# Sparse attention's start: bias table in two head groups, the first scores ahead of the compression, the root ahead of gelu, biases one head ahead

## The chip, the cores and the metric

One core of a Trainium2 chip runs the whole program. The metric is device time in microseconds (us) of one execution; three executions of the kernel before gave 3542.86, 3545.63 and 3548.09, median 3545.63.

## What is computed

Three layers of a decoder, all in fp32: a first block with a recurrent branch and sparse attention beside each other, then two blocks more. The change lies in the sparse attention of the first block alone (256 tokens, 16 heads of 64 in four key groups):

```python
kc = compress(k_c, pe_k, w1_k, w2_k)      # gelu(windows of 32 tokens @ w1) @ w2, 15 windows
vc = compress(v_c, pe_v, w1_v, w2_v)
s_c = einsum('bsgrd,bngd->bgrsn', q, kc) * scale + bias_c    # compressed scores
p_c = softmax(where(valid_c, s_c, NEG_INF)) * any_c
o_c = einsum('bgrsn,bngd->bsgrd', p_c, vc)
s = einsum('bgrqk', qc, ks) * scale + bias[rel_bucket(dist)] # selected blocks: all four of them here
o_s = softmax(where(dist >= 0, s, NEG_INF)) @ vs
o_w = ...                                                     # window attention, the same form
o = gate0 * o_c + gate1 * o_s + gate2 * o_w
```

With 256 tokens every block is selected and the window covers all, so a head has two score tables of 256 by 256 (causal: 128 + 256 columns for two blocks of queries), and one compressed table of 256 by 15. The recurrent branch ends in an RMS norm (a sum of squares over eight tiles, a root, a reciprocal, a scaling), and both branches go into the product with w_out.

## The kernel before, in words

The program is one list of instructions for each engine, tied by semaphores. The large products take their weights in quarters of 128x1024: SyncE loads a quarter (`w_raw`), ScalarE rounds it (`w_hi`, function `hi`), VectorE subtracts (`w_lo`, function `lo`), TensorE uses both; each step waits for the step ahead and for its buffer (four quarters deep). The pair of weight tiles `in1` makes the projections; the two pairs of `cmp` (c0 and c0 + 1) hold the first weights of the key and the value compression; `out1` is the product behind attention.

Between `in1` and `out1` the order is written by hand:

- SyncE loads the bias table `bias` (128 x 16 heads x 384, 3 MB from a Toeplitz copy in HBM, eight DMAs) behind all eight quarters of `cmp`. Its place was the input of `in1`, so it waits until that is used up.
- TensorE turns the values to tokens, multiplies 96 small products of the compression (m0, m1), turns the gelu results (`turn_hidden`), sums the squares of the recurrent branch (`lru_sum`), makes the scores of head pair 0 (`pair_scores`), the second compression product, and the compressed scores of all heads. `keep_busy` is a row of products whose result nobody reads.
- ScalarE rounds the quarters, squares the recurrent tiles, then gelu (`hidden`), the copies of it, the root of the norm, and a table of exp. Each change of function family loads a table.
- VectorE adds biases to the scores of a head (two instructions of 128x384), takes maxima (two), and negates them; ScalarE takes exp of the head (four instructions with sums); VectorE then makes the reciprocal and the factor and scales the head in place; TensorE transposes it; ScalarE copies it (`pt_att`); after each pair TensorE multiplies with the values (`pair_results`). This is a loop over `it`, written out on all three engines: in step `it` VectorE scores head `it` and scales head `it` - 1. In step 0 VectorE also does the whole softmax of the compressed scores (`compressed`).

`lru_n` and `z` are tiles of the recurrent branch, `s_first` and `s_more` the scores of even and odd pairs, `p_cmp` the compressed scores, `stat` small statistics. Score banks hold one pair: m0 and m1, and bank0 and bank1.

## Time and profile before

| | us |
|---|---|
| median of three executions | 3545.63 |
| lowest, highest | 3542.86, 3548.09 |
| the profiled execution's own time | 3545.68 |
| its span | 3543.9 |
| from the start of the compression products to the first product of `out1` | 249.99 to 342.31 |

The stage that the change touches is less than 100 us of the span. Elsewhere TensorE's large products set the time; here the engines hand small work to each other, so it must be read from the order of time, the waits and the chain. `SPq` is SyncE's queue. `x4` at the end of a row is the number of instructions in it, and what stands in brackets is the idle time before and what ended it. An fp32 product appears as two instructions, and four exps of a head as eight (each with a read of its sum).

### The profile page before, as it was taken

To read this page: it belongs to the slowest core of one execution; us is meant where nothing else is said; L and a number is where in the kernel's file an instruction comes from. 1 tells how busy PE (TensorE), PEld (TensorE's weight loads), DVE (VectorE), ACT (ScalarE), POOL (GpSimd) and SP (SyncE) were. 2 spreads that over 40 slices of the span, in tenths; PEclk is the share of its full clock that TensorE was granted. 3 is DMA by queue.
4 is the path that set the end of the run, shared out by engine and by line. 5 is a ranking of instruction groups with operands and counts; after the bars stand their busy time and mean duration, and the time that the engine had idled before them with its cause. 6 is when DMAs were issued, how large, how long until landed. Compare 5 with 4: busy or idle time off the path is not lost.

```text
span 3543.9 us, 62898 instructions
## 1 busy us (share of the span) xinstructions
PE 3438.5 (97%) x21968; PEld 2998.0 (85%) x21968; DVE 2297.3 (65%) x3449; ACT 1788.3 (50%) x2742; POOL 489.5 (14%) x538
## 2 busy tenths in 40 slices
PE   9998999999999999999999999999489999999999
PEld 7886888888888888887888888888378888888888
DVE  5788565555555766775666677778855765565565
ACT  4477464545454554553555444444444554444454
POOL 0001410111114100123100001105012000001105
PEclk9999999999999999999999999999899999999999
DMA  6562545565556555553456556667235455555555
GB/s 212 172 184 61 190 151 192 186 191 185 190 183 194 170 188 170 162 168 119 145 193 197 187 189 196 202 222 246 59 125 186 147 190 191 185 187 193 181 187 195
DMA packets 190644, 626.52 MB, mean 177 GB/s; under 512 B 26822, under 2 KB 40328, under 8 KB 190360
## 3 DMA queue, kind: packets, MB, share of 16 engines
q1 hardware_dynamic: 179948, 612.29, 53.9%
q10 hardware_dynamic: 10572, 12.56, 1.2%
q8 instruction: 80, 1.31, 0.2%
q14 instruction: 44, 0.36, 0.0%
HBM read 620.32 MB, written 3.15 MB: 176 GB/s over the span
## 4 chain that ended last, share of the span: by engine, by line
PE 88%; DVE 7%; ACT 2%; DMA 1%; issue 1%; POOL 0%; SPq 0%; ACTq 0%; DVEq 0%; POOLq 0%
PE bank L1943 54%; PE bank L1946 28%; PE m L1966 1%; DVE w_lo L1073 1%; DMA w_raw<-stream 1%; PE m L1956 1%; PE m L1968 1%; DVE prod L1749 1%; ACT w_hi L481 0%; DVE st L1752 0%; DVE st L1754 0%; DVE y L1100 0%; DVE w_lo L1077 0%; ACT s_first L666 0%; ACT u_own L972 0%
## 5 line engine op out<-in xcount | busy, mean ns | idle before, releaser
L1073 DVE TENSOR_TENSOR w_lo<-w_raw,w_hi 128x1024 fp32r<-128x1024 f32 x1086 | 1336.4, 1253 | 776.5 <-ACT w_hi L481 770.2
L1943 PE MATMUL bank<-act,w_hi 128*128 128x512 f32 x6016 | 1512.8, 393 | 3.6 <-DVE w_lo L1073 1.6
L481 ACT ACTIVATE w_hi<-w_raw 128x1024 fp32r<-128x1024 f32 x1090 | 1129.5, 1054 | 409.8 <-PE bank L1946 362.6
L1943 PEld LDWEIGHTS bank<-act,w_hi 128*128 128x128 f32 x6016 | 1082.7, 189 | 204.6 <-DVE w_lo L1073 4.3
L1946 PEld LDWEIGHTS bank<-act,w_lo 128*128 128x128 f32 x6016 | 820.8, 190 | 58.9
L1946 PE MATMUL bank<-act,w_lo 128*128 128x256 f32 x6016 | 838.7, 282 | 0.0
L1943 PE MATMUL bank<-ffn,w_hi 128*128 128x512 f32 x2432 | 613.5, 393 | 4.0 <-DVE w_lo L1077 2.7
L490 ACT ACTIVATE low<-bank 128x256 f32<-128x256 f32 x542 | 207.5, 383 | 745.0 <-PE bank L1946 744.1
L1943 PEld LDWEIGHTS bank<-ffn,w_hi 128*128 128x128 f32 x2432 | 436.2, 189 | 83.2 <-DVE w_lo L1077 5.0
L1946 PEld LDWEIGHTS bank<-ffn,w_lo 128*128 128x128 f32 x2432 | 333.9, 190 | 25.1
L1081 DVE TENSOR_TENSOR ev<-bank,low 128x256 f32<-128x256 f32 x468 | 198.2, 423 | 236.7 <-ACT low L490 233.3
L1946 PE MATMUL bank<-ffn,w_lo 128*128 128x256 f32 x2432 | 341.5, 282 | 0.0
L1852 POOL TENSOR_TENSOR ffn<-fv,ffn 128x256 f32 x152 | 113.4, 746 | 1547.8 <-ACT ffn L738 1123.0
L1867 POOL TENSOR_TENSOR y<-y,ev 128x256 f32 (+1 forms) x109 | 92.3, 847 | 369.9 <-DVE ev L1081 369.9
L1835 POOL TENSOR_TENSOR sq<-y 128x256 f32<-128x256 f32 x90 | 95.2, 1058 | 315.9 <-DVE y L1786 226.6
L738 ACT ACTIVATE ffn<-fv 128x256 f32 (+1 forms) x88 | 36.8, 418 | 148.4 <-DVE fv L1389 148.4
L1837 POOL TENSOR_TENSOR ssum<-ssum,sq 128x256 f32<-128x256 f32 x90 | 105.9, 1177 | 7.1
L1966 PE MATMUL m<-act,w_hi 128*128 128x512 f32 x224 | 84.3, 458 | 4.0 <-DVE act L1197 2.5
L735 ACT ACTIVATE sg<-ev 128x256 f32<-128x256 f32 x88 | 36.9, 419 | 96.3 <-DVE ev L1384 96.3
L1077 DVE TENSOR_TENSOR w_lo<-w_raw,w_hi 128x768 fp32r<-128x768 f32 x58 | 67.9, 1187 | 21.5 <-ACT w_hi L486 21.2
L1384 DVE TENSOR_TENSOR ev<-ev,rms 128x256 f32<-128x256 f32 x176 | 74.8, 425 | 6.0
L1081 DVE TENSOR_TENSOR y<-bank,low 128x256 f32 (+1 forms) x74 | 31.4, 424 | 64.6 <-ACT low L490 64.6
(425 smaller groups left out, 2236.8 us busy)
## 6 DMA issues: line engine op xcount, KB each, us to landing
w_raw<-stream SPq DMA_DIRECT2D x1148, 512.0 KB, 3.5
b_part<-s_bt ACTq DMA_DIRECT2D x16, 256.0 KB
bias<-toeplitz SPq DMA_DIRECT2D x4, 512.0 KB, 9.1
pow_b<-powers ACTq DMA_DIRECT2D x8, 256.0 KB
pow_b<-powers ACTq DMA_DIRECT2D x16, 128.0 KB
res<-x_t SPq DMA_DIRECT2D x2, 512.0 KB, 9.0
res<-x_t ACTq DMA_DIRECT2D x2, 512.0 KB, 11.0
bias<-toeplitz SPq DMA_DIRECT2D x4, 256.0 KB, 11.7
```

Of the source, the lines that this page charges most:

```text
L481: a(w_hi[:, q, :], w_raw[:, q, :], ACT.Copy).then_inc(hi_ready, 1)
L490: a(low[:, w, 0:n], src[w][:, n:2 * n], ACT.Copy).then_inc(low_copied, 1)
L1073: e.tensor_tensor(w_lo[:, q, :], w_raw[:, q, :], w_hi[:, q, :].bitcast(F32), ALU.subtract).then_inc(lo_ready, 1)
L1081: e.tensor_tensor(dst, src[w][:, 0:n], low[:, w, 0:n], ALU.add).then_inc(drained, 1)
L1384: e.tensor_tensor(ev[:, w, :], ev[:, w, :], rms[:, :], ALU.mult).then_inc(sem(("gate_scaled", "up_scaled")[w]), 1)
L1835: e.tensor_tensor(sq[:, k % 2, :], y[:, k, :], y[:, k, :], ALU.mult).then_inc(y_squares, 1)
L1837: e.tensor_tensor(ssum[:, :], ssum[:, :], sq[:, k % 2, :], ALU.add).then_inc(y_squares, 1)
L1852: e.tensor_tensor(ffn[:, tile, T:2 * T], fv[:, w, :], ffn[:, tile, 0:T].bitcast(F32), ALU.subtract).then_inc(f_ready, 1)
L1867: e.tensor_tensor(y[:, 2 * i + w, :], y[:, 2 * i + w, :], ev[:, w, :], ALU.add).then_inc(y_acc, 1)
L1943: mm(bank[w][:, 0:2 * n], w_hi[:, q, wt], x(h * hk + k, 0, 2 * n), start=(h == 0 and k == 0), stop=False)
L1946: last = mm(bank[w][:, n:2 * n], w_lo[:, q, wt], x(h * hk + k, 0, n), start=False, stop=(h == 1 and k == hk - 1))
L1966: mm(m[w][:, :], w_hi[:, 2 * w + h, wt], act[:, k, :], start=(k == 0), stop=False)
```

## The change

- `bias` is loaded in two groups of heads: heads 0 to 3 directly behind the first quarter of the second `cmp` pair, heads 4 to 15 behind its fourth. The first group counts on the semaphore `bias_steps`, which the load of `rev_hot` now uses too.
- TensorE makes the scores of pair 0 ahead of the compression products, those of pair 1 behind the sums; the compression writes to one bank (m4), the gate transposes to m5. Three of the eight squares are summed ahead of the last quarter, five behind it. The compressed scores are made in two halves, around the transposes of head 0. `keep_busy(22)` and `keep_busy(10)` are gone.
- ScalarE takes the root of the recurrent norm ahead of gelu, and loads the table of exp ahead of the copies of gelu's results. The copies of the compressed keys and values come behind exp of head 0, exp of the compressed scores behind exp of head 3.
- VectorE scores head 0 ahead of the loop and head `it` + 1 in step `it`. The softmax of the compressed scores is cut in two, in steps 2 and 3. `lo(c0, 3)` and `lo(c0 + 1, 0)` move ahead of one other instruction each.
- The transposes of the compressed weights (`cmp_weights`) come behind heads 2, 3, 5, 7, ... 15 instead of 0, 2, 4, ... 14.

```diff
+    FIRST_HEADS = 4
+    TURN_AFTER = (2,) + tuple(range(3, NH, 2))
...
-            with sp_eng.Fori(2, after_in1) as i:
+            with sp_eng.Fori(2, after_in1 - 1) as i:
                 for q in range(4):
                     sp_eng.wait_ge(lo_ready, 4 * i + (q - 3))
                     load(i, q)
-            sp_eng.wait_ge(halves_used, 4 * PH["in1"][1])
-            sp_eng.wait_ge(sem("toep_out"), 16)
-            for lo_c, hi_c, off in ((128, 384, 127), (0, 128, 255)):
-                for p0 in range(0, P, ROWS):
-                    src = bass.AP(toeplitz.tensor, off - p0, [[383, ROWS], [384 * ROWS, NH], [1, hi_c - lo_c]])
-                    sp_eng.dma_start(bias[p0:p0 + ROWS, :, lo_c:hi_c], src).then_inc(sem("bias_loaded"), 16)
+
+            def load_bias(h0, h1, into):
+                for lo_c, hi_c, off in ((128, 384, 127), (0, 128, 255)):
+                    for p0 in range(0, P, ROWS):
+                        src = bass.AP(toeplitz.tensor, off - p0 + 384 * ROWS * h0,
+                                      [[383, ROWS], [384 * ROWS, h1 - h0], [1, hi_c - lo_c]])
+                        sp_eng.dma_start(bias[p0:p0 + ROWS, h0:h1, lo_c:hi_c], src).then_inc(into, 16)
+
+            for q in range(4):
+                sp_eng.wait_ge(lo_ready, 4 * (after_in1 - 1) + (q - 3))
+                load(after_in1 - 1, q)
+                if q == 0:
+                    sp_eng.wait_ge(halves_used, 4 * PH["in1"][1])
+                    sp_eng.wait_ge(sem("toep_out"), 16)
+                    load_bias(0, FIRST_HEADS, sem("bias_steps"))
+            load_bias(FIRST_HEADS, NH, sem("bias_loaded"))
...
+            hi(c0 + 1, 0)
             block_high(1)
...
-                a(hid_t[:, kv, :], m[kv][0:NG * NCMP, 0:T], ACT.Gelu_apprx_tanh).then_inc(sem("hid_ready"), 1)
+                a(hid_t[:, kv, :], m[4][0:NG * NCMP, T * kv:T * kv + T], ACT.Gelu_apprx_tanh).then_inc(sem("hid_ready"), 1)
...
-            hi(c0 + 1, 0)
+            hi(c0 + 1, 1)
+            hi(c0 + 1, 2)
             lru_square(0, 3)
-            hi(c0 + 1, 1)
-            lru_square(3, 6)
-            hi(c0 + 1, 2)
-            lru_square(6, 8)
             hi(c0 + 1, 3)
+            lru_square(3, 8)
+            root_table()
+            norm("lru", z, 8, lru_n, LT * P, None)
             hidden(0)
             hidden(1)
             a(counted[:, 0:1], eps_col[:, :], ACT.Copy).then_inc(low_copied, 4)
+            a(exp_use[:, :], eps_col[:, :], ACT.Exp)
             for kv in range(2):
                 s.wait_ge(sem("cmp_mm"), kv + 1)
                 a(hid[:, kv, :, :], m[2 + kv][:, 0:2 * NG * NCMP].rearrange("p (f n) -> p f n", f=2), ACT.Copy).then_inc(sem("cmp_cp"), 1)
-            root_table()
-            s.wait_ge(sem("blk_ready"), 1)
-            s.wait_ge(sem("cmp_mm"), 3)
-            for h in range(2):
-                pr = slice(64 * h, 64 * h + 64)
-                a(k_cmp[pr, :, h, :], m[4][pr, 0:60].rearrange("p (a h n) -> p a h n", a=2, h=2)[:, :, h, :],
-                  ACT.Copy).then_inc(sem("cmp_cp"), 1)
-            a(v_cmp[:, :], m[4][0:NCMP, 64:320], ACT.Copy).then_inc(sem("cmp_cp"), 1)
-            norm("lru", z, 8, lru_n, LT * P, None)
-            a(exp_use[:, :], eps_col[:, :], ACT.Exp)
+
+            def compressed_copies():
+                s.wait_ge(sem("blk_ready"), 1)
+                s.wait_ge(sem("cmp_mm"), 3)
+                for h in range(2):
+                    pr = slice(64 * h, 64 * h + 64)
+                    a(k_cmp[pr, :, h, :], m[4][pr, 0:60].rearrange("p (a h n) -> p a h n", a=2, h=2)[:, :, h, :],
+                      ACT.Copy).then_inc(sem("cmp_cp"), 1)
+                a(v_cmp[:, :], m[4][0:NCMP, 64:320], ACT.Copy).then_inc(sem("cmp_cp"), 1)
 
...
-                if hh % 2 == 0:
-                    s.wait_ge(sem("pct_mm"), hh // 2 + 1)
-                    a(pt_cmp[:, (hh // 2) % 2, :, :], m[5][0:NCMP, :].rearrange("n (h t) -> n h t", h=2),
+                if hh in TURN_AFTER:
...
                 if it == 0:
+                    compressed_copies()
+                if it == 3:
                     s.wait_ge(sem("cmp_vec"), 3)
...
             block_low(0)
+            c0 = PH["cmp"][0]
+            lo(c0, 3)
             v.wait_ge(sem("lru_act"), 4)
             v.wait_ge(sem("lru_vec"), 12)
             e.tensor_tensor(z[:, 0:LT, :], lru_i[:, :, :], z[:, LT:2 * LT, :], ALU.mult).then_inc(sem("lru_vec"), 1)
-            c0 = PH["cmp"][0]
-            lo(c0, 3)
+            lo(c0 + 1, 0)
             block_low(1)
-            lo(c0 + 1, 0)
             for q in range(1, 4):
...
             e.memset(counted[:, 1:2], 0.0).then_inc(drained, 4)
 
...
                 e.tensor_tensor(pc, pc, stat[:, 0:32].unsqueeze(2).to_broadcast([P, 32, NCMP]), ALU.subtract).then_inc(sem("cmp_vec"), 2)
+
+            def compressed_weights():
+                pc = p_cmp[:, :, :]
                 v.wait_ge(sem("cmp_exp"), 1)
...
-                v.wait_ge(sem("tok_cp"), 3)
...
+            def score(hh):
+                if hh == 0:
+                    v.wait_ge(sem("bias_steps"), 16 + 32 * P // ROWS)
+                if hh == FIRST_HEADS:
+                    v.wait_ge(sem("bias_loaded"), 32 * P // ROWS)
+                if hh >= 4:
+                    v.wait_ge(sem("pt_mm"), 2 * hh - 6)
+                for at_ in range(2):
+                    v.wait_ge(sem("s_mm"), 4 * (hh // 2) + 2 * at_ + hh % 2 + 1)
+                    e.scalar_tensor_tensor(s_att(hh)[:, at_, :], score_bank[hh % 2][at_][:, 0:384], HD ** -0.5, bias[:, hh, :],
...
+            v.wait_ge(sem("tok_cp"), 3)
+            score(0)
+            top(0)
+            top_negated(0)
             for it in range(NH + 1):
...
+                o = (it + 1) % 2
+                if it + 1 < NH:
+                    score(it + 1)
                 if it:
                     v.wait_ge(sem("att_exp"), it)
                     e.reciprocal(stat[:, 112 + 8 * o:116 + 8 * o], stat[:, 96 + 8 * o:100 + 8 * o]).then_inc(sem("att_inv"), 1)
-                if it < NH:
-                    v.wait_ge(sem("s_bias"), 2 * it + 2)
-                    e.tensor_reduce(stat[:, 80 + 8 * b:82 + 8 * b], s_att(it)[:, :, 0:128], AX.X, ALU.max).then_inc(sem("att_top"), 1)
-                    e.tensor_reduce(stat[:, 82 + 8 * b:84 + 8 * b], s_att(it)[:, :, 128:384], AX.X, ALU.max).then_inc(sem("att_top"), 1)
+                if it + 1 < NH:
+                    top(it + 1)
                 if it:
                     v.wait_ge(sem("att_inv"), it)
...
-                if it == 0:
-                    compressed()
+                if it + 1 < NH:
+                    top_negated(it + 1)
+                if it == 3:
+                    compressed_weights()
                 if it == 3:
                     lo(c0 + 2, 0)
...
+                if it == 2:
+                    compressed_scores()
                 if it == 3:
...
+            pe.wait_ge(sem("lru_sig"), 2 * LT)
+            pair_scores(0)
...
+                into = m[4][0:60, T * kv:T * kv + T]
+                for q in range(4):
+                    if kv and q == 3:
+                        pe.wait_ge(sem("tok_cp"), 3)
+                        lru_sum(0, 3)
+                    pe.wait_ge(lo_ready, 4 * i + q + 1)
...
+            lru_sum(3, 8)
+            pair_scores(1)
...
             turn_hidden(0)
-            lru_sum(0, 2)
             turn_hidden(1)
-            pair_scores(0)
             pe.wait_ge(sem("cmp_cp"), 2)
-            pe.wait_ge(sem("tok_cp"), 3)
...
                               cols[:, w2v + 64 * f:w2v + 64 * f + 64], start=(f == 0), stop=(f == 1))
             last.then_inc(sem("cmp_mm"), 1)
-            lru_sum(2, 8)
-            pe.wait_ge(sem("cmp_cp"), 5)
...
                 for j in range(NH // 2):
                     last = mm(m[4][:, 30 * (8 * b + j):30 * (8 * b + j + 1)], z[:, 16 + j, 128 * b:128 * b + 128],
                               k_cmp[:, j // 4, :, :].rearrange("p h n -> p (h n)"), start=True, stop=True)
-            last.then_inc(sem("cmp_scores"), 1)
-            keep_busy(22)
+                if b:
+                    last.then_inc(sem("cmp_scores"), 1)
 
...
             def transposes(hh):
-                if hh == 1:
-                    keep_busy(10, m[4])
...
             for it in range(NH + 2):
+                if it == 1:
+                    compressed_scores(0)
+                if it and it % 2 == 0 and it + 2 < NH:
+                    pair_scores(it // 2 + 1)
                 if 1 <= it <= NH:
-                    if it % 2:
-                        cmp_weights(it // 2)
+                    if it - 1 in TURN_AFTER:
+                        cmp_weights(TURN_AFTER.index(it - 1))
                     transposes(it - 1)
-                if it % 2 == 0 and it + 2 < NH:
-                    pair_scores(it // 2 + 1)
+                if it == 1:
+                    compressed_scores(1)
                 if it == NH:
```

On **SyncE**, between the last quarters of `cmp` and those of `out1`. Before:

```order
L405 DMA w_raw<-stream 128x1024
L422 REGISTER_ALU
L422 COMPARE_AND_BRANCH
L431 DMA bias<-toeplitz 32x16x256 x4
L431 DMA bias<-toeplitz 32x16x128 x4
L432 UNCONDITIONAL_BRANCH
L432 ISA
L405 ISA
L405 DMA w_raw<-stream 128x1024
```

And in the change:

```order
L407 DMA w_raw<-stream 128x1024
L424 REGISTER_ALU
L424 COMPARE_AND_BRANCH
L407 DMA w_raw<-stream 128x1024
L434 DMA bias<-toeplitz 32x4x256 x4
L434 DMA bias<-toeplitz 32x4x128 x4
L407 DMA w_raw<-stream 128x1024 x3
L434 DMA bias<-toeplitz 32x12x256 x4
L434 DMA bias<-toeplitz 32x12x128 x4
```

A quarter of 0.5 MB, then eight DMAs of four heads (0.75 MB), the three other quarters, then eight of twelve heads (2.25 MB).

On **ScalarE**, from gelu of the compression (`hid_t`) to the first exp. Before:

```order
L631 ACT_TABLE_LOAD
L631 ACTIVATE hid_t<-m 60x256 x2
L645 ACTIVATE counted<-eps_col 128x1
L648 ACTIVATE hid<-m 128x120 x2
L525 ACT_TABLE_LOAD
L525 ACTIVATE no_use<-eps_col 128x1
L654 ACTIVATE k_cmp<-m 64x2x15 x2
L656 ACTIVATE v_cmp<-m 15x256
L514 ACTIVATE rms<-m,eps_col 128x256
L658 ACT_TABLE_LOAD
L658 ACTIVATE exp_use<-eps_col 128x1
L666 ACTIVATE s_first,stat<-s_first,stat 128x128
```

And in the change, from behind the last square:

```order
L537 ACT_TABLE_LOAD
L537 ACTIVATE no_use<-eps_col 128x1
L526 ACTIVATE rms<-m,eps_col 128x256
L644 ACT_TABLE_LOAD
L644 ACTIVATE hid_t<-m 60x256 x2
L658 ACTIVATE counted<-eps_col 128x1
L659 ACT_TABLE_LOAD
L659 ACTIVATE exp_use<-eps_col 128x1
L662 ACTIVATE hid<-m 128x120 x2
L679 ACTIVATE s_first,stat<-s_first,stat 128x128
```

The root (`rms`) stood behind everything of the compression and now stands ahead of gelu; the tables come in the order root, gelu, exp instead of gelu, root, exp. The copies of `k_cmp` and `v_cmp` have gone behind exp of head 0.

On **TensorE**, behind the compression products. `hid_t` is turned, `hid` and `cols` are the second product, `k_cmp` makes the compressed scores, L2027 is `keep_busy`. Before:

```order
L2151 MATMUL m<-hid,cols 128x60 x2
L2154 MATMUL m<-cols,hid 15x64 x8
L2121 MATMUL m<-lru_n,ones 128x256 x6
L2161 MATMUL m<-k_cmp,z 128x30 x16
L2027 MATMUL m<-ident,ones 128x128 x22
L2132 MATMUL m<-z 128x256
L2132 MATMUL bank<-z 128x256
```

And in the change:

```order
L2187 MATMUL m<-ident,hid_t 128x60 x4
L2194 MATMUL m<-hid,cols 128x60 x2
L2197 MATMUL m<-cols,hid 15x64 x8
L2204 MATMUL m<-k_cmp,z 128x30 x8
L2229 MATMUL m<-ident,s_first 128x128 x6
L2204 MATMUL m<-k_cmp,z 128x30 x8
L2142 MATMUL m<-z 128x256
L2142 MATMUL bank<-z 128x256
```

The sums (L2121 before) have gone ahead of these rows, the compressed scores come in two halves with head 0's transposes between them, and nothing keeps the array busy.

On **VectorE**, around the second half of the compressed softmax. Before (in step 0):

```order
L1350 TENSOR_SCALAR stat<-stat 128x4
L1310 SCALAR_TENSOR_TENSOR p_cmp<-m,bias_cmp 128x480
L1312 TENSOR_REDUCE stat<-p_cmp 128x32
L1314 TENSOR_TENSOR p_cmp<-p_cmp,stat 128x480
L1316 TENSOR_REDUCE stat<-p_cmp 128x32
L1317 RECIPROCAL stat<-stat 128x32
L1320 TENSOR_SCALAR g_tok<-g_tok,cols 128x16
L1321 TENSOR_TENSOR stat<-stat,g_tok 128x32
L1323 TENSOR_TENSOR p_cmp<-p_cmp,stat 128x480
L1335 SCALAR_TENSOR_TENSOR s_first<-bank,bias 128x384 x2
L1338 RECIPROCAL stat<-stat 128x4
```

And in the change (in step 3):

```order
L1381 TENSOR_TENSOR stat<-stat,g_tok 128x4
L1362 TENSOR_SCALAR stat<-stat 128x4
L1335 TENSOR_REDUCE stat<-p_cmp 128x32
L1336 RECIPROCAL stat<-stat 128x32
L1337 TENSOR_SCALAR g_tok<-g_tok,cols 128x16
L1338 TENSOR_TENSOR stat<-stat,g_tok 128x32
L1340 TENSOR_TENSOR p_cmp<-p_cmp,stat 128x480
L1089 TENSOR_TENSOR w_lo<-w_raw,w_hi 128x1024
L1394 TENSOR_TENSOR s_more<-s_more,stat 128x2x128
L1394 TENSOR_TENSOR s_more<-s_more,stat 128x2x256
```

The five instructions that end with the write of `p_cmp` now stand behind the bias and the maxima of head 4, ahead of the scaling of head 2 (`s_more`).

## Rows read from the trace of the kernel before

**Rows 1.** The page of the kernel before: its head and the shares of the chain.

```profile
span 3543.9 us, 62898 instructions
...
PE 88%; DVE 7%; ACT 2%; DMA 1%; issue 1%; POOL 0%; SPq 0%; ACTq 0%; DVEq 0%; POOLq 0%
```

**Rows 2.** The chain that ended last, 236 to 345 us: start, length, what.

```profile
249.93 2.20 DVE z L1298
...
254.03 0.35 SPq L431
...
262.51 10.29 DMA bias<-toeplitz
...
282.23 1.87 ACT s_first L666 x8
```

**Rows 3.** Waits, 236 to 345 us: in total, times, longest.

```profile
DVE s_first L1335 <- DMA bias<-toeplitz: 11.5, 1, 11.5
...
ACT s_first L666 <- DVE stat L1350: 9.2, 4, 4.5
```

**Rows 4.** Order of time on TensorE: start, length, operation, idle before.

```profile
246.63 1.09 PE L2095 MATMUL m<-ident,z 128*128 128x128 f32 x8 [1.88 <-DVE z L1213]
...
249.99 0.47 PE L2112 MATMUL m<-w_hi,blk_s 128*60 128x256 f32 x1 [2.26 <-DVE blk_s L1293]
...
263.61 0.28 PE L2114 MATMUL m<-w_hi,blk_s 128*60 128x256 f32 x1
...
268.35 2.86 PE L2121 MATMUL m<-lru_n,ones 128*128 128x256 f32 x12
...
271.04 3.65 PE L2161 MATMUL m<-k_cmp,z 128*128 128x30 f32 x32
```

**Rows 5.** Order of time on ScalarE, the same columns.

```profile
261.38 0.38 ACT L631 ACTIVATE hid_t<-m 60x256 f32<-60x256 f32 x1
...
271.25 0.47 ACT L514 ACTIVATE rms<-m,eps_col 128x256 f32<-128x256 f32 x1 [1.92 <-PE m L2121]
...
271.74 1.28 ACT L658 ACT_TABLE_LOAD   x1
...
273.03 0.20 ACT L658 ACTIVATE exp_use<-eps_col 128x1 f32<-128x1 f32 x1
...
275.20 0.40 ACT L666 ACTIVATE s_first<-s_first,stat 128x128 f32<-128x128 f32 x1 [1.97 <-DVE stat L1350]
```

**Rows 6.** Order of time on VectorE, the same columns.

```profile
272.83 1.02 DVE L1335 SCALAR_TENSOR_TENSOR s_first<-m,bias 128x384 f32<-128x384 f32 x2 [11.50 <-DMA bias<-toeplitz]
...
273.89 0.42 DVE L1341 TENSOR_REDUCE stat<-s_first 128x2 f32<-128x256 f32 x1
...
274.23 0.68 DVE L1342 TENSOR_REDUCE stat<-s_first 128x2 f32<-128x512 f32 x1
...
277.79 0.65 DVE L1316 TENSOR_REDUCE stat<-p_cmp 128x32 f32<-128x480 f32 x1 [0.67 <-ACT p_cmp L698]
...
335.27 0.18 DVE L1338 RECIPROCAL stat<-stat 128x4 f32<-128x4 f32 x1 [1.00 <-ACT s_more L666]
...
335.69 1.03 DVE L1359 TENSOR_TENSOR s_more<-s_more,stat 128x256 f32<-128x256 f32 x2
```

**Rows 7.** Stretches: length, then PE, PEld, DVE, ACT, POOL busy, granted clock, DMA, GB/s.

```profile
251.00:252.00 1.00, 1.00 (x7) 1.00 (x6) 1.00 (x1) 0.66 (x2) 0.00 (x0) 0.50 0.87 336
...
254.00:255.00 1.00, 1.00 (x7) 1.00 (x7) 0.92 (x2) 1.00 (x3) 0.00 (x0) 0.60 0.60 66
...
277.00:278.00 1.00, 1.00 (x6) 1.00 (x6) 0.33 (x2) 0.67 (x2) 0.00 (x0) 0.50 0.00 0
...
290.00:291.00 1.00, 0.00 (x0) 0.00 (x0) 1.00 (x3) 1.00 (x5) 0.00 (x0) 1.00 0.00 0
...
293.00:294.00 1.00, 1.00 (x8) 0.62 (x10) 1.00 (x4) 0.00 (x0) 0.00 (x0) 0.50 0.16 45
...
295.02:302.25 7.23, 6.42 (x58) 4.29 (x54) 7.05 (x21) 7.09 (x24) 0.00 (x0) 0.95 0.00 1
```

83 lines of the change are left out of this document (42 added, 41 removed).

## The prediction

> **What bounds the kernel now.** I read the page's chain first: 88% of it is TensorE [rows 1], so over the span only TensorE's rate and its waits count. The change lies in less than 100 us between two large products, so I then read the chain inside that stage [rows 2], the waits [rows 3] and the order of time on three engines [rows 4 to 6]. One wait stands out: VectorE stands 11.5 us in front of the first biased score, until the bias table is there at 272.83 [rows 3, 6]. The chain goes back from it over the transfer (10.29 us behind the last of eight issues) to SyncE's first bias issue at 254.03 [rows 2]. That issue stands behind the last quarter of `cmp`, which waits for the low part of c0's last quarter, and this is behind the 2.20 us product on `z` [rows 2].
>
> Is the wait worth 11.5 us? Only if everything else that head 0 needs is there sooner. ScalarE takes the root at 271.25 and loads the table of exp until 273.02 [rows 5]. So with the table in place at once, exp of head 0 (275.20 before) could start at 273.2 at best: 2.0 us, and the rest of the 11.5 us is cover for ScalarE's and TensorE's chain. More can come only from edits that shorten that chain.
>
> Behind the start, the loop over heads fills two engines: in 7.23 us (two heads) VectorE is busy 7.05 and ScalarE 7.09 [rows 7]. Nothing of it can be gained by order, only its beginning and its end. ScalarE's waits for VectorE (9.2 us in four waits) [rows 3] lie at the beginning, and cost something only where VectorE itself isn't full.
>
> **Term A, the start of exp of head 0.** The compression products start when the first low part of `blk_s` is there; nothing ahead of that moves, so they start near 250 again [rows 4]. The scores of pair 0 now stand in the 2.26 us in which TensorE waits there [rows 4]: free. The products end at 263.9 [rows 4]. Eight sums are to be made before the root, six of which take 2.69 us (268.35 to 271.04) [rows 4], so 0.45 each and 3.6 for all: three ahead of the last quarter, five behind it, all on TensorE's path. End: 267.5. Then ScalarE: root 0.47, table of gelu 1.28, two gelus of 0.38, a small copy and the table of exp with its first use, 1.48, two copies of about 0.2 (all but the last in [rows 5]): 4.3 us, so 271.8. Against 275.20 that is 3.4 us earlier. A further gain is possible: the first products run at the lower level of the clock (granted 0.50 at 251, which is 1.2 GHz, and rising within the microsecond at 254) [rows 7], after 1.88 and 2.26 us of idle [rows 4]. With pair 0's scores in one of these gaps the clock may rise as early as 251, over 3 us sooner, which gives back half of that, 1.7 us (an estimate from these two rows). Bounds of A: 3.4 to 5.1 us; I take 4.3, the middle, since no row shows this stretch filled.
>
> The root's move puts two table loads into the open between the root and the first exp, where one stood before; that is in the sum. ScalarE's row shows 1.28 us for a load, and the next instruction starts 0.01 us behind it [rows 5]. The Trainium skill ("ScalarE: Activation LUTs", What ACT_TABLE_LOAD costs) puts a switch at about 2.66 us, since a drain of 1.38 comes on top. This speaks against the change: by it A would be smaller by 2.8 us; the trace shows no such drain, and the sum goes by the row.
>
> **Term B, from exp of head 0 to the end of the last scaling.** Before: 275.20 to 336.72, 61.5 us [rows 5, 6]. VectorE works through almost all of it: from 272.83 to 336.72, 63.9 us, of which it idles 0.67 for exp of the compressed scores, 1.00 for the last head [rows 6] and 0.18 in each pair of heads [rows 7], with smaller pieces about 3.1. So it has 60.8 us of work. Ahead of the end of exp of head 0 it can now do three heads' biases (1.06 each) and two heads' maxima (1.10) [rows 6]: 5.4. With exp itself (1.87) [rows 2] the stretch is 1.9 + 55.4 = 57.3 at the least, 4.2 less than before, if VectorE never waits again.
>
> It will wait, at three places. In step 3 exp of the compressed scores now stands behind exp of head 3 on ScalarE, and VectorE asks for it right behind the maxima of head 4; queued behind that wait are the low part for `out1`, the scaling of head 2 and so head 2's transposes: about 1.5 us (it was 0.67 behind head 0) [rows 6]. In steps 15 and 16 VectorE has no head left to score, and two scalings come faster than ScalarE can deliver two exps with their copies; I take 2.5 us for 1.00 before [rows 6]. In the steps with a high part on ScalarE the transposes now stand behind the next pair's scores, which delays copies and the next exp: some 1.6 us over four pairs. Sum 5.6, and B is 57.3 + 5.6 = 62.9: a loss of 1.4. Bounds: gain 4.2, loss 3.
>
> **Term C, the clock of TensorE.** The change takes 32 filler products out. Before, after the compressed scores (30 columns a product, 3.65 us) [rows 4] the clock fell: 0.50 granted at 277, although TensorE was busy throughout [rows 7]. It fell again to 0.50 at 293, behind an idle stretch at 290 [rows 7]. In the change TensorE meets: a wait for two gelus behind the root, one for the copies, one for the copies of the keys (behind exp of head 0), the same products of 30 columns in two halves, then a wait of some 6 us from head 1's transposes to the compressed weights. I expect a low clock from about 272 on. On the path of heads 0 and 1 TensorE has the second product, the compressed scores and two heads' transposes, some 6.5 us; if half is caught, it grows by 3.2, of which VectorE has about 0.8 to spare: a loss of 2.4. Bounds: 0 and 4.2 (all caught, some saved elsewhere). Before, the drop at 277 lay on fillers alone and cost nothing.
>
> The Trainium skill ("TensorE: Matmul & The Clock Gate", Part 1) says that "the default state is throttled, and activity releases the throttle"; by it C would be at its upper bound, since the activity here is thin. The row at 277, a fall in the middle of filler after thin products, agrees.
>
> **The transfers.** Bias group one (0.75 MB) starts some 8 us sooner than 254.03, right behind one quarter, and is there long before 261. Three quarters now stand behind its eight issues on SyncE; the first issues took 0.35 us [rows 2], so they come 3 to 4 us later. ScalarE wants them from 255.4 on: tight, but covered, as TensorE is the one that ends last there. Group two is issued from about 252.5, 1.5 us before the whole table was before, with a quarter less in it; head 4 asks for it at about 280. No cost.
>
> **Sum.** -4.3 + 1.4 + 2.4 = -0.5 us. On the profiled execution's 3545.68 (span 3543.9 [rows 1] and what lies around it), which lies at the median of 3545.63, this gives **3545.2 us**.
>
> **The rivals.**
> - *The clock holds* (C = 0, A = 5.1): -5.1 + 1.4 = -3.7, 3542.0. For it: the products at 271 to 274.5 ran at full clock while it lasted [rows 4]. Against it: the new waits. 0.22.
> - *VectorE never waits* (A = 5.1, B = -4.2): -9.3, 3536.4; with half of the three waits -6.5, 3539.2. For it: VectorE is the fuller engine before. Against it: ScalarE is as full [rows 7]. 0.12, of which 0.08 is below 3538.5.
> - *A low clock in the loop*, slower than before. TensorE is busy 6.42 of 7.23 us in a pair of heads [rows 7]; its work now comes in one piece, transposes, results and next scores, with one idle piece of 2 to 3 us instead of several short ones, as long as those behind which the clock fell [rows 4, 7]. A low stretch like that from 251 to 254 costs half its length, 1.7 us, since the next scores then come late for VectorE. It decides from the second such stretch on: two give -0.5 + 3.4, 3548.6; four 3552. 0.18, of which 0.05 is above 3552.7.
> - *The quarters come late* behind the eight issues, by up to 3 us, on TensorE's path: 3548.2. 0.04.
> - The forecast has what is left, 0.44, with 3543 to 3547.5 as its own range.
>
> **The range.** From half of "never waits" to three low stretches: 3538.5 to 3550.5; the three executions themselves lie 5.2 us apart. About 0.2% (7.1 us) is what a measurement of this kernel can tell from no change. Faster by more than that (under 3538.5): 0.08. Slower (over 3552.7): 0.06. Within: 0.86.
>
> **What would show it.** Right if in the profile after: the 11.5 us wait for the table is gone and VectorE's longest wait in the stage is for exp of head 0, 4 us or more; that exp starts between 270 and 272; VectorE waits 1 to 2 us for exp of the compressed scores and 2 to 3 for the last head; the granted clock is 0.50 somewhere between 272 and 290; the first product of `out1` starts within 2 us of 342.3. Wrong if ScalarE waits over 1 us for a quarter near 256 (transfers), if the loop has several microseconds at 0.50 (third rival), or if it ends before 338 (second rival).

## The result: 8 us slower

Median time after: 3553.28 us (13 runs, 3549.2 to 3557.56), before in the same comparison: 3545.07 us (13 runs). Ratio 1.0023, 95% interval 1.0015 to 1.0030: slower by 8.2 us (5.3 to 10.6). Forecast were 3545.2 us and a range of 3538.5 to 3550.5, so the time lies outside it. In the comparison of the last four runs below, one execution of the kernel before took 4245.9 us at a mean granted clock of 0.749 (0.988 to 0.993 in the others), and it is left out of every difference. Page of the profile of the kernel after, head and shares of the chain [rows 1]:

```profile
span 3551.3 us, 62764 instructions
...
PE 89%; DVE 6%; ACT 2%; DMA 2%; issue 1%; POOL 0%; ACTq 0%; SPq 0%; DVEq 0%; POOLq 0%
```

Waits of the kernel after, 244 to 356 us: in total, times, longest [rows 3].

```profile
ACT pt_cmp L687 <- PE m L2217: 10.0, 4, 3.5
ACT pt_att L691 <- PE m L2229: 8.7, 3, 4.7
...
DVE stat L1376 <- ACT s_first L679: 6.8, 5, 4.1
...
PE m L2217 <- DVE p_cmp L1340: 6.1, 1, 6.1
...
DVE s_more L1350 <- PE bank L2145: 5.2, 4, 1.9
ACT w_hi L493 <- DMA w_raw<-stream: 5.1, 4, 2.1
...
DVE p_cmp L1326 <- PE m L2204: 4.3, 1, 4.3
...
DVE stat L1335 <- ACT p_cmp L714: 3.4, 1, 3.4
```

The 11.5 us wait for the bias table is gone. In its place stand waits in a ring: VectorE for ScalarE's exps (6.8 in five waits) and for scores, ScalarE for transposes, TensorE for the compressed weights (a ring, since each of the three engines waits for work that depends on the other two). New too is ScalarE's wait for quarters of the weight (`w_raw`).

Chain of the kernel after [rows 2], start, length, what; then the issues on SyncE; and, for the last quarter of `cmp`, the time from its issue to its landing before (issued at 253.43), with the kernel after in the first line of the chain (10.32):

```profile
252.83 10.32 DMA w_raw<-stream
...
267.15 2.17 PE m L2157 x10
```

```profile
247.10 3.70 SPq L434 DMA_DIRECT2D bias<-toeplitz  x8
250.84 2.32 SPq L407 DMA_DIRECT2D w_raw<-stream  x3
253.20 14.61 SPq L434 DMA_DIRECT2D bias<-toeplitz  x8
```

```profile
w_raw<-stream SPq DMA_DIRECT2D x1, 512.0 KB, 4.1
```

Order of time after: TensorE [rows 4], ScalarE [rows 5], VectorE [rows 6].

```profile
277.63 3.62 PE L2204 MATMUL m<-k_cmp,z 128*128 128x30 f32 x16 [0.95 <-ACT v_cmp L671]
...
282.38 3.46 PE L2204 MATMUL m<-k_cmp,z 128*128 128x30 f32 x16
...
296.29 1.01 PE L2217 MATMUL m<-ident,p_cmp 128*15 128x128 f32 x4 [6.12 <-DVE p_cmp L1340]
...
355.95 0.73 PE L2002 MATMUL m<-act,w_hi 128*128 128x512 f32 x2
```

```profile
245.70 0.38 ACT L518 ACTIVATE low<-bank 128x256 f32<-128x256 f32 x1 [1.73 <-PE bank L1982]
...
269.35 0.47 ACT L526 ACTIVATE rms<-m,eps_col 128x256 f32<-128x256 f32 x1 [2.07 <-PE m L2157]
269.84 1.28 ACT L644 ACT_TABLE_LOAD   x1
271.13 0.65 ACT L644 ACTIVATE hid_t<-m 60x256 f32<-60x256 f32 x2
...
273.59 0.40 ACT L679 ACTIVATE s_first<-s_first,stat 128x128 f32<-128x128 f32 x1
...
283.01 0.39 ACT L679 ACTIVATE s_more<-s_more,stat 128x128 f32<-128x128 f32 x1
...
289.57 1.13 ACT L691 ACTIVATE pt_att<-m 128x384 f32<-128x384 f32 x2 [4.71 <-PE m L2229]
...
300.24 0.39 ACT L679 ACTIVATE s_first<-s_first,stat 128x128 f32<-128x128 f32 x1
```

```profile
285.88 0.66 DVE L1326 SCALAR_TENSOR_TENSOR p_cmp<-m,bias_cmp 128x480 f32<-128x480 f32 x1 [4.30 <-PE m L2204]
...
293.92 0.65 DVE L1335 TENSOR_REDUCE stat<-p_cmp 128x32 f32<-128x480 f32 x1 [3.37 <-ACT p_cmp L714]
...
348.92 0.18 DVE L1376 RECIPROCAL stat<-stat 128x4 f32<-128x4 f32 x1 [2.10 <-ACT s_more L679]
```

Exp of head 0 starts at 273.59 (before 275.20), but `out1`'s first product comes at 355.95 (before 342.31). From here on I measure the **stage** from the start of `in1`'s last small copy on ScalarE (244.85 before, 245.70 after) to `out1`'s first product: 97.5 before, 110.3 after, 12.8 more. The rows at 283.01 and 300.24 are the starts of exp of heads 2 and 4, 17.2 us apart; before they are 9.6 apart:

```profile
285.45 0.40 ACT L666 ACTIVATE s_more<-s_more,stat 128x128 f32<-128x128 f32 x1
...
295.02 0.40 ACT L666 ACTIVATE s_first<-s_first,stat 128x128 f32<-128x128 f32 x1 [2.31 <-DVE stat L1350]
```

From exp of head 0 to exp of head 6 it is 37.4 us against 27.1 before, from there to exp of head 14 32.6 against 27.9. So most of the loss lies in the first six heads. Stretches of the kernel after [rows 7] (length; PE, PEld, DVE, ACT, POOL busy; clock; DMA; GB/s):

```profile
251.00:254.00 3.00, 3.00 (x26) 2.76 (x26) 2.42 (x2) 1.81 (x4) 0.00 (x0) 1.00 1.09 183
270.00:273.00 3.00, 1.39 (x16) 0.98 (x12) 1.11 (x2) 2.97 (x5) 0.00 (x0) 1.00 1.20 216
275.00:280.00 5.00, 4.05 (x27) 3.78 (x26) 3.78 (x12) 2.94 (x13) 0.00 (x0) 0.50 0.68 273
280.00:285.00 5.00, 5.00 (x25) 5.00 (x26) 1.57 (x5) 2.72 (x10) 0.00 (x0) 0.50 0.02 3
...
295.00:300.00 5.00, 2.73 (x12) 1.82 (x14) 4.93 (x8) 1.22 (x3) 0.00 (x0) 0.50 0.30 103
```

TensorE runs at 0.50 (1.2 GHz) from 273.5 to 290.5, 294 to 304, 318 to 321 and 335 to 338: 33 us together against 13.5 before (counted in steps of half a microsecond).

**Where 5 us came back.** The span grew by 7.4 us only. From `out1`'s first product on, the parts between ScalarE's table loads take the same time in both traces to within half a microsecond, but for one, between these two:

```profile
2416.28 1.28 ACT L537 ACT_TABLE_LOAD   x1
...
2580.84 1.28 ACT L1016 ACT_TABLE_LOAD   x1
```

That is 164.6 us, against 170.1 in the profiled execution of before (2402.83 to 2572.97). In that stretch the chain goes over four or five transfers of `w_raw` at some 7 to 8 us each, and over the 18 profiles of this study it took 164.6 to 170.1 us. It may carry most of what the runs of one kernel differ by; with one profile for each kernel this is not shown. So the stage of one profile and the median of runs may differ by several us, and both are given below. In all 17 comparisons the median's difference lies under the stage's, by 0.2 to 6.4 us. One reason may be that all stages are compared with the one profile of before, which has the longest such stretch. Whether the change also shortens it stays open: before_no_fill and before_split, which keep the old loop, took 168.0 and 168.9, the 15 others 164.6 to 169.9.

### The profile page after: what moved, and what is told of

It reads as the page before. It is cut to its first block, busy times and chain, and to the rows that moved or that the text cites. A ratio compares the mean times of both kernels' runs of the same rounds, so it can differ in the third digit from the quotient of the medians.

```text
span 3551.3 us, 62764 instructions
## 1 busy us (share of the span) xinstructions
PE 3438.5 (97%) x21904; PEld 2995.7 (84%) x21904; DVE 2299.3 (65%) x3449; ACT 1787.9 (50%) x2742; POOL 489.0 (14%) x538
## 4 chain that ended last, share of the span: by engine, by line
PE 89%; DVE 6%; ACT 2%; DMA 2%; issue 1%; POOL 0%; ACTq 0%; SPq 0%; DVEq 0%; POOLq 0%
PE bank L1979 54%; PE bank L1982 28%; PE m L2002 1%; DMA w_raw<-stream 1%; DVE w_lo L1089 1%; PE m L1992 1%; PE m L2004 1%; DVE prod L1785 1%; ACT w_hi L493 0%; DVE y L1116 0%; DVE st L1788 0%; DVE st L1790 0%; DVE w_lo L1093 0%; ACT u_own L988 0%; PE m L2419 0%
## 5 line engine op out<-in xcount | busy, mean ns | idle before, releaser
L1982 PEld LDWEIGHTS bank<-ffn,w_lo 128*128 128x128 f32 x2432 | 333.8, 190 | 25.2
L1093 DVE TENSOR_TENSOR w_lo<-w_raw,w_hi 128x768 fp32r<-128x768 f32 x58 | 68.1, 1189 | 19.5 <-ACT w_hi L498 19.3
L1097 DVE TENSOR_TENSOR y<-bank,low 128x256 f32 (+1 forms) x74 | 31.4, 424 | 64.5 <-ACT low L502 64.5
## 6 DMA issues: line engine op xcount, KB each, us to landing
bias<-toeplitz SPq DMA_DIRECT2D x4, 384.0 KB, 13.5
```

Source lines behind the costliest of these rows:

```text
L1097: e.tensor_tensor(dst, src[w][:, 0:n], low[:, w, 0:n], ALU.add).then_inc(drained, 1)
L1982: last = mm(bank[w][:, n:2 * n], w_lo[:, q, wt], x(h * hk + k, 0, n), start=False, stop=(h == 1 and k == hk - 1))
```

## Experiments

Each is compared with the kernel before on the same chip. All times (column us) are differences of medians to it. The kernels ran on different chips, so two rows are compared by their differences, and where their intervals of the ratio overlap the order of the two is not shown by the times. Theory 1: late quarters. Theory 2: TensorE's low clock. Theory 3: the order of the steps. All at once first:

| run | us | ratio, 95% | exp 0 | loop | stage | low |
|---|---|---|---|---|---|---|
| before | 0 | | 30.4 | 61.5 | 97.5 | 13.5 |
| the change | +8.2 | 1.0015-1.0030 | 27.9 | 76.8 | 110.3 | 33 |
| quarters_first | +5.5 | 1.0005-1.0023 | 25.4 | 78.1 | 109.1 | 40 |
| fill_start | +6.3 | 1.0009-1.0027 | 27.0 | 71.4 | 104.0 | 13.5 |
| fill_loop | +8.0 | 1.0014-1.0032 | 26.8 | 73.5 | 105.9 | 30.5 |
| before_no_fill | -0.7 | 0.9989-1.0007 | 30.8 | 62.1 | 98.5 | 20.5 |
| exp_early | +4.3 | 1.0004-1.0022 | 26.5 | 73.4 | 105.5 | 34 |
| turn_first | +14.8 | 1.0029-1.0056 | 26.8 | 86.3 | 118.7 | 50 |
| mended | +8.5 | 1.0018-1.0039 | 25.2 | 78.2 | 108.9 | 24 |
| before_split | +0.1 | 0.9989-1.0007 | 30.1 | 63.3 | 100.6 | 13.5 |
| own_step | +2.7 | 1.0000-1.0018 | 25.4 | 68.9 | 101.7 | 27 |
| own_step_filled | -3.8 | 0.9983-1.0001 | 27.7 | 65.4 | 98.8 | 10.5 |
| filled | +5.0 | 1.0004-1.0022 | 26.6 | 70.4 | 103.1 | 13.5 |
| best | -10.3 | 0.9961-0.9980 | 25.4 | 60.1 | 92.3 | 3.5 |
| best_late | -7.6 | 0.9969-0.9987 | 28.0 | 60.5 | 95.2 | 3 |
| best_bare | -0.1 | 0.9991-1.0009 | 25.4 | 68.1 | 100.3 | 30 |
| best_softmax_late | -6.0 | 0.9975-0.9994 | 25.4 | 62.3 | 94.5 | 6.5 |
| best_one_ahead | -4.8 | 0.9981-0.9999 | 25.4 | 63.1 | 94.1 | 3.5 |

"exp 0" is its start behind `in1`'s last small copy; "loop" runs from there to the end of the last scaling; "low" is the time at 0.50. The last four columns are of one profiled execution each, in us.

**quarters_first.** The first bias group goes behind all four quarters.

```diff
             for q in range(4):
                 sp_eng.wait_ge(lo_ready, 4 * (after_in1 - 1) + (q - 3))
                 load(after_in1 - 1, q)
-                if q == 0:
-                    ...
-                    load_bias(0, FIRST_HEADS, sem("bias_steps"))
+            ...
+            load_bias(0, FIRST_HEADS, sem("bias_steps"))
             load_bias(FIRST_HEADS, NH, sem("bias_loaded"))
```

> The changed kernel with one edit: the first bias group is issued behind all four quarters of the second compression weight instead of behind its first quarter. The changed kernel stood 8.2 us above the kernel before (3553.3 against 3545.1). Theory 1 (late quarters): ScalarE's four waits for quarters, 5.1 us, go, the compression products end some 3 us sooner than 267.2, exp of head 0 starts near 270.5, and the time falls by 3 us, to about +5 us against the kernel before. Theory 2 (low clock of TensorE behind thin products and idle time) and theory 3 (the new order of the steps) say that the loss lies behind exp of head 0: there the stretch from that exp to the first product of out1 stays at 82 us against 67 before. A rival to theory 1: the quarters' lateness is covered by the sums and table loads, under 1 us gained.

ScalarE no longer waits for quarters, exp of head 0 comes 2.5 us sooner, and the time is 2.7 us lower by the medians, with intervals that overlap. By the trace theory 1 holds, and something is left for theories 2 and 3: the loop stayed long (78.1), and this execution had 40 us of low clock.

**fill_start**, **fill_loop.** Fillers (`keep_busy`) where TensorE idles, first in the beginning, then in the loop.

```diff
             pair_scores(1)
+            keep_busy(3)
...
             turn_hidden(1)
+            keep_busy(6, m[5])
             pe.wait_ge(sem("cmp_cp"), 2)
...
+            keep_busy(7, m[5])
...
+                    keep_busy(20, m[5])
                     pe.wait_ge(sem("cmp_p"), 1)
...
+                if hh == 1:
+                    keep_busy(6, m[5])
```

```diff
+                elif hh >= 4 and hh % 2 == 0:
+                    pe.wait_ge(sem("pct_cp"), hh // 2)
+                    keep_busy(5, m[5])
```

> The changed kernel with filler products back on TensorE where it idles at the stage's beginning: 3 behind the scores of pair 1, 6 behind the transposes of the gelus, 7 behind the second product, 6 ahead of head 1's transposes, 20 ahead of the first compressed weights. Theory 2 (clock): the granted clock no longer stays at 0.50 from 273.7 to 290.2; the 32 products of the compressed scores take about 3.6 us instead of 6.9, the two heads' transposes 1.8 instead of 2.9, VectorE's wait for the compressed scores falls from 4.3 to about 1 us, and the time falls by 3 to 4 us (to +4 or +5 against the kernel before). Theory 1 and theory 3: the time stays within 1 us of the changed kernel's +8.2.

> The changed kernel with 5 filler products ahead of the transposes of heads 4, 6, ... 14, where TensorE idles 1.6 and 2.3 us in turn. Theory 2 (clock): the low stretches at 294 to 304, 318 to 321 and 335 to 338 go or become fewer, a pair of heads takes 7.5 to 7.6 us instead of 7.5 to 9.0, and the time falls by 3 to 4.5 us. Theory 3 (the order itself): pairs stay above 8 us even where the clock is 1.00, and the time stays within 1 us of +8.2. Theory 1: no effect.

fill_start: the long low stretch is gone, VectorE's wait for the compressed scores is 0.5 instead of 4.3, the stage is 6.3 shorter. By the medians only 1.9 of the 3 to 4 us expected came of it, within the error of both. Its trace shows what stays at mostly full clock: 4.4 us of VectorE's waiting for exp of the compressed scores, and ScalarE's 4.4 us for head 1's transposes:

```profile
285.29 0.87 ACT L691 ACTIVATE pt_att<-m 128x384 f32<-128x384 f32 x2 [4.39 <-PE m L2235]
...
289.37 0.65 DVE L1335 TENSOR_REDUCE stat<-p_cmp 128x32 f32<-128x480 f32 x1 [4.38 <-ACT p_cmp L714]
```

fill_loop: no low stretch in the loop behind 302, no pair of heads behind head 6 over 7.9 us (the change had two of over 9), the stage 4.4 shorter, the median unchanged (+8.0), where 3 to 4.5 less were expected. By the median nothing is shown. By the trace the four pairs from exp of head 6 to exp of head 14 take 29.3 us, against 32.6 in the change and 27.9 before: here the clock costs 3.3 us and the order 1.4.

**before_no_fill.** In the kernel before, `keep_busy(22)` and `keep_busy(10, m[4])` are taken out.

> The kernel before with one part of the change alone: its 22 and 10 filler products behind the compressed scores and ahead of head 1's transposes are taken out. Theory 2 (clock): the clock falls to 0.50 for 10 us or more behind 275 and the loop begins later: the first product of out1 comes 2 to 4 us after 342.3, time +2 to +4 us. Theories 1 and 3: no effect, within 1 us of the kernel before.

The clock did fall, from 277 to 287, and cost nothing that can be measured (2 to 4 us were expected by theory 2, which missed here; the stage is 1.1 longer). The old order seems to have room for it. So the removal of the fillers is no cause by itself.

**exp_early.** `if it == 3:` becomes `if it == 2:` in front of ScalarE's exp of the compressed scores.

> The changed kernel with one move: exp of the compressed scores stands in ScalarE's step 2 (behind exp of head 2, ahead of head 1's copies) instead of step 3. Theory 3 (what is queued behind a wait in steps 2 and 3): VectorE's wait of 3.4 to 4.4 us for this exp falls under 1 us, the scaling of head 2 and its transposes come some 3 us sooner, and the stretch from the end of in1 to the first product of out1 falls from 110.3 by 2 to 3.5 us; by the median of runs about +5.5 against the kernel before instead of +8. Theories 1 and 2: no effect, or the clock stays low as long as before and takes the gain (under 1 us).

+4.3 instead of +8.2 (the intervals just overlap), with the clock as low as in the change (34 us). VectorE's wait for this exp (3.4) is gone. The stage is 4.8 shorter, but 1.4 of it lies ahead of exp of head 0, where the edit changes nothing; the loop is 3.4 shorter. One line is worth 3 to 4 us: theory 3.

**turn_first.** TensorE's order is put back, the transposes ahead of the next pair's scores.

```diff
-                if it and it % 2 == 0 and it + 2 < NH:
-                    pair_scores(it // 2 + 1)
                 if 1 <= it <= NH:
                     if it - 1 in TURN_AFTER:
                         cmp_weights(TURN_AFTER.index(it - 1))
                     transposes(it - 1)
+                if it and it % 2 == 0 and it + 2 < NH:
+                    pair_scores(it // 2 + 1)
```

> The changed kernel with the order of TensorE's steps put back: the transposes of a head stand ahead of the next pair's scores, as before the change. Theory 3: ScalarE's waits for the transposes (4.7 us for head 1's) and VectorE's waits for scores (1.4 to 1.9 us in every second pair) go; a pair of heads takes 7.2 to 7.4 us instead of 7.5 to 9.0, and the stretch from in1's end to out1's first product falls from 110.3 by 5 to 8 us. Theory 2: the idle time of TensorE is cut into shorter pieces, so low stretches in the loop go with it; from 273.7 to 290 the clock stays low all the same. Theory 1: no effect.

A clear miss: 15 us slower than before. VectorE's waits, 300 to 350 us, and one of them in order of time:

```profile
DVE s_more L1350 <- PE bank L2145: 8.5, 3, 3.8
DVE s_first L1350 <- PE bank L2145: 6.9, 2, 4.1
```

```profile
314.46 1.14 DVE L1350 SCALAR_TENSOR_TENSOR s_first<-m,bias 128x384 f32<-128x384 f32 x2 [4.08 <-PE bank L2145]
```

I had taken the scores' new place for the fault; it is what makes biases one head ahead bearable. Theory 3 had to be put otherwise: it is slack. VectorE asks for a pair's first scores one head sooner than before. In between, TensorE has to do an even head's transposes, the results of the pair before, and only then these scores. In the kernel after this is, first at full clock, then with the clock at 0.50 from 317.8 to 321.2:

```profile
308.21 0.87 PE L2229 MATMUL m<-ident,s_first 128*128 128x128 f32 x6 [1.63 <-DVE s_first L1394]
...
312.55 0.61 PE L2217 MATMUL m<-ident,p_cmp 128*15 128x128 f32 x4
...
316.10 0.87 PE L2229 MATMUL m<-ident,s_more 128*128 128x128 f32 x6 [2.29 <-DVE s_more L1394]
...
322.07 0.61 PE L2217 MATMUL m<-ident,p_cmp 128*15 128x128 f32 x4
```

4.3 us and 6.0 us, where VectorE's step is 3.6 (half of 7.23). So VectorE waits for scores in every second pair, TensorE idles 1.6 to 2.3 us behind it, and behind idle times of 2.3 us the clock fell at 317.8 and at 334.8 (fill_loop, which fills these gaps, has no such fall). Order and clock feed each other.

**mended** joins quarters_first, exp_early, turn_first and fillers of 3, 6, 7 and 6.

> The changed kernel with all that helps by the theories: quarters of the second compression weight ahead of the first bias group, exp of the compressed scores in step 2, transposes ahead of the next scores, and fillers of 3, 6, 7 and 6 products around the gelus, the second product and the compressed weights. If late quarters (3 us), the clock at the start (3 to 6) and the order (5 to 8) are the whole loss, in1's end to out1's first product takes 94 to 98 us, against 97.5 in the kernel before and 110.3 in the changed one: a time between -3 and +1 us of the kernel before. If something else is in it, it stays above 100 us.

+8.5, a miss: -3 to +1 was expected. By the trace it is turn_first that spoilt it: VectorE waits 14.7 us for scores, against 17.3 in turn_first and 5.5 in the change. No run takes turn_first alone out of it. Its exp of head 0 is the earliest of all.

**before_split.** The kernel before with the two bias groups placed as in the change, nothing else.

> The kernel before with one part of the change alone: the bias table in two head groups, the first behind the first quarter of the second compression weight. VectorE's wait of 11.5 us in front of the first biased score goes. The prediction's first step says it is worth at most 2.0 us, as the root and the table of exp end at 273.0 and exp of head 0 starts at 275.2; theory 1 says that the late quarters (3 us later) then move the products, the sums and the root by up to 3 us. So: exp of head 0 within 1 us of where it was, in1's end to out1's first product 97 to 98.5 us, the time within 1 us of the kernel before. A rival: the wait was worth more, -3 us or better.

+0.1. VectorE's 11.5 us wait has turned into two others (its waits, 244 to 285 us):

```profile
DVE p_cmp L1321 <- PE m L2174: 6.1, 1, 6.1
...
DVE s_first L1348 <- PE m L2148: 4.1, 1, 4.1
```

The wait that stood out most was worth nothing that can be measured alone, in line with the prediction's first step (at most 2.0 us). But the late quarters come with this edit, so a gain of up to 2.0 and their cost may hide each other; no run has the early bias group in the old kernel without them. The stage was 3.1 us longer than before in this profile, 100.6 where 97 to 98.5 was expected; the median shows nothing of it.

**own_step**, **own_step_filled.** Put back together: TensorE's order (the diff of turn_first) and, from head 5 on, VectorE's scoring of a head in its own step. The second adds fillers: 3, 6, 7, 5, 12, and 3 in each later pair.

```diff
-                if it + 1 < NH:
-                    score(it + 1)
+                new = it + 1 if it < AHEAD else it if AHEAD < it < NH else None
+                if new is not None:
+                    score(new)
```

> The changed kernel with VectorE's loop and TensorE's order put back together: biased scores are one head ahead for heads 1 to 4 alone, VectorE's step 4 scores none, from head 5 on each head is scored in its own step; the transposes stand ahead of the next pair's scores. Putting TensorE's order back alone made it 15 us slower than the kernel before. Theory 3, as that run mends it (slack): with biases one head ahead, TensorE must fit an even head's transposes (0.87 us), the results of the pair before (some 2.6) and the next pair's scores (1.7) between that head's scaling and VectorE's next but one step, 5.1 us in a step of 3.6, and the weights and transposes of the odd head too where they stand ahead. In its own step a pair's scores have a whole step more. So VectorE's waits for scores go (in the run with the transposes first they were 2.8 to 4.1 us in each pair), a pair takes 7.2 to 7.6 us, the stretch from in1's end to out1's first product falls from 118.7 to about 104 to 107, and the time to +4 to +7 us. A rival (the loss in the loop is the clock alone): the clock still falls in the loop's idle time and the stretch stays above 110.

> The run with heads 5 to 15 in their own steps, plus fillers on TensorE: 3 behind pair 1's scores, 6 and 7 around the second product, 5 ahead of head 1's transposes, 12 ahead of the first weights, 3 in each later pair. Theory 2 and 3 together (low clock at the start, slack in the loop): the stretch falls a further 3 to 5 us, to 100 to 103, the time to +2 to +4. If theory 3 alone holds, the fillers bring nothing, or cost up to 1 us.

+2.7 and -3.8, both better than expected (+4 to +7, +2 to +4). Compared with turn_first only VectorE's order differs, and that is 12 us: with the transposes first it is slack that was missing. VectorE waits 3.3 us for scores instead of 17.3. The wait for exp of the compressed scores is gone as well, as it is in turn_first, though the softmax stands where the change has it. The fillers are worth another 6.5 by the medians, 2.9 by the stage.

**filled.** The change's order with fillers everywhere (3, 6, 7, 6, 24, and 8 in each later pair).

> The changed kernel, its order untouched, with fillers everywhere it idles: 3, 6, 7, 6 at the start as before, 24 ahead of the first weights, 8 ahead of the transposes of heads 4, 6, ... 14. It measures the price of the order at (nearly) full clock. Theory 2 (the clock is all of the loss): the stretch falls from 110.3 to 99 or less and the time to within 1 us of the kernel before. Theories 2 and 3 (the clock is some half of it): the stretch is 102 to 104, the time +4 to +5 us. Eight fillers (1.8 us) may fill more than the idle time of 1.6 us and cost 0.2 us a pair.

+5.0 and a stage of 103.1, both as expected by theories 2 and 3, with a low time of 13.5 us as in the kernel before. What is left is the order and the late quarters. VectorE still waits 4.3 us for exp of the compressed scores here.

**best.** quarters_first, own_step, the whole of the compressed scores ahead of head 0's transposes, their softmax in step 2, weights turned behind heads 2, 4, ... 14 and 15, and the fillers of own_step_filled. ScalarE's part:

```diff
+                if it == 2:
+                    s.wait_ge(sem("cmp_vec"), 3)
+                    a(p_cmp[:, :, :], p_cmp[:, :, :], ACT.Exp).then_inc(sem("cmp_exp"), 1)
                 if it < NH:
                     att_exp(it)
```

> All mends together, by the order as read: quarters ahead of the first bias group; heads 5 to 15 in their own steps, transposes first; the whole of the compressed scores ahead of head 0's transposes, their softmax in step 2 (exp ahead of head 2's, weights behind head 1's scaling), which is VectorE's and ScalarE's emptier time; weights turned at even heads as in the kernel before; the same fillers. If late quarters, clock and slack are the whole of the loss, only the gain of the change's start (exp of head 0 some 5 us sooner than the kernel before) is left: the stretch is 93 to 96 us against 97.5, a time of -5 to -2 us, 3540 to 3543. If something else is in it, the stretch is above 98.

-10.3 us against the kernel before (3535.5 us, ratio 0.9970), 18 under the change. The stage, 92.3, is 5.2 under before, about what was expected (93 to 96); the median is 5 us better than expected (-5 to -2), and where this second half comes from is the open question of the result's last paragraph. The rows of best: `in1`'s last small copy and exp of head 0, the compressed scores, `out1`, and two stretches.

```profile
244.43 0.38 ACT L518 ACTIVATE low<-bank 128x256 f32<-128x256 f32 x1 [1.73 <-PE bank L1983]
...
269.86 0.40 ACT L679 ACTIVATE s_first<-s_first,stat 128x128 f32<-128x128 f32 x1
```

```profile
273.27 3.65 PE L2208 MATMUL m<-k_cmp,z 128*128 128x30 f32 x32
```

```profile
336.70 0.73 PE L2003 MATMUL m<-act,w_hi 128*128 128x512 f32 x2
```

```profile
275.00:280.00 5.00, 3.73 (x34) 3.54 (x33) 4.03 (x10) 1.77 (x6) 0.00 (x0) 1.00 0.05 18
280.00:285.00 5.00, 4.94 (x45) 4.57 (x46) 4.86 (x14) 4.91 (x18) 0.00 (x0) 1.00 0.00 2
```

The clock is full where the change had 0.50, and VectorE and ScalarE are full again from 280 on.

**One mend taken back at a time**, from best. best_late: the first bias group behind the first quarter again. best_bare: no fillers. best_softmax_late: compressed scores in halves and their softmax in steps 2 and 3, as in the change. best_one_ahead: biases one head ahead through all heads, scores ahead of the transposes, weights at odd heads.

> The best version (3535.5, 10.3 us under the kernel before; in1's end to out1's first product 92.3 us) with one mend taken back: the first bias group is issued behind the first quarter again, as in the change. Theory 1: ScalarE waits 2.5 to 5 us for quarters, exp of head 0 starts 1.5 to 2.5 us later (26.8 to 27.9 us behind in1's end, instead of 25.4), and all of it stays on the path: +1.5 to +2.5 us against the best version. A rival: behind exp of head 0 ScalarE or VectorE has slack that takes it up, under 0.7 us.

> The best version without its fillers (3, 6, 7, 12, 5 and 3 in each later pair). Theory 2: the clock falls to 0.50 from about 272 for 10 us or more, the compressed scores take 6 to 7 us instead of 3.7, and the stretch grows from 92.3 to 97 to 101 us, +5 to +8 us. If slack in the order alone was the cause (theory 3), the order of the best version bears the low clock: under +3 us.

> The best version with the softmax of the compressed scores where the change has it: products in two halves around head 0's transposes, vector part behind step 2, exp behind exp of head 3, weights ahead of the scaling in step 3. Theory 3, first part (what is queued behind VectorE's wait for this exp): VectorE waits 3 to 4 us for it, head 2's scaling and transposes stand behind it, +4 to +6 us. A rival: with the clock at full it is worth under 2 us.

> The best version with the loop as the change has it: biased scores one head ahead through all heads, the next pair's scores ahead of the transposes, weights turned at odd heads. Theory 3, second part (slack): at full clock a pair takes 7.5 to 7.6 us instead of 7.2, VectorE waits 0.8 to 1.5 us for scores in a part of the pairs, and the stretch grows by 2 to 4 us. Where the clock falls in the loop, a pair takes up to 9 us and it is 5 or more. A rival: the early softmax has removed all of it, under 1 us.

Prices against best, by the medians (each uncertain by 4 to 5 us, as best ran on another chip than these four and each is compared with the kernel before on its own) and by the stage: late quarters 2.7 and 3.0; low clock 10.2 and 8.0; late softmax 4.3 and 2.3; one head ahead 5.5 and 1.8. By the times only the low clock and one head ahead are clear of noise: the other two intervals overlap that of best. All four sum to 23 and 15; the change lies 18 above best.

Two prices are not made of what was expected. In best_softmax_late VectorE waits only 0.4 us for exp of the compressed scores (3 to 4 were expected, 4.3 it is in filled). exp_early and turn_first, one edit each from the change, have no such wait. So it needs both: the softmax late, and the next pair's scores ahead of the transposes. In best_one_ahead the loop is 3.0 us longer, and the last three heads take 1.7 of it (VectorE waits 2.7 us in them, 1.0 in best); waits for missing slack are 1.3. From the last scaling to `out1` it is then 1.2 shorter, which leaves 1.8. Its profile had no low clock in the loop. Its runs spread more widely than the others' (3534.2 to 3544.5); the mean granted clock was 0.989 to 0.991 in the four longest and 0.991 to 0.992 in the seven others, so the clock may have fallen in the loop in some, but no trace shows it.

## Why the prediction was wrong

In short: the new start brought what was forecast of it, less what the late quarters took; the loop over heads behind it took 15 us more than before, where 1.4 and 2.4 were forecast for order and clock.

**What bounds it: right, as far as shown.** Without the 11.5 us wait the old kernel took the same time (before_split, +0.1, with the late quarters in it).

**Term A: right but for the quarters.** With them first, exp of head 0 starts 25.2 to 25.4 us behind `in1`'s last small copy in six profiles, 4.9 to 5.2 sooner than before: about the upper end of 3.4 to 5.1. The gain at the clock came true as well: it was 1.00 from 251 to 254, where before it was 0.50. The table loads took 1.28 us each and the next instruction came 0.01 behind; the drain of 1.38 us that the Trainium skill ("ScalarE: Activation LUTs", What ACT_TABLE_LOAD costs) puts on a switch isn't seen here, as weighed.

**Transfers: "No cost" was the first failing step.** It counted the issue delay on SyncE (3 to 4 us, measured 3.7) and called it covered, since TensorE "is the one that ends last there". It isn't: TensorE then waits for the quarters' low parts (2.3 us). And the delay was the smaller part. The last quarter was issued no later than before (252.83, before 253.43), but took 10.3 us to land instead of 4.1 (5.0 in quarters_first, where no bias group is issued ahead of it). The likely reason is that the group's 0.75 MB share the DMA engines with it, which were busy throughout from 251 to 254 (a share of 1.09): the working had no term for this. The Trainium skill ("DMA: Bandwidth & Descriptors", Queues, rings and completion order) says that each DMA engine takes the descriptors of one queue in ring order, but that completion is not first in, first out. The order in a ring is not in the trace, nor when the first group landed. With the second half a trace agrees: in best_late a bias transfer issued 0.4 us behind the last quarter landed 2 us ahead of it. How long the last quarter takes also varies at the same order of issues: 7.0 us in own_step, whose exp of head 0 came at 25.4. With group one behind the first quarter, nine profiles have that exp at 25.4 to 28.0, 1.6 later on the mean than the six with quarters first. So the rival with a chance of 0.04 was a part of what happened, though by the times of the runs (2.7 us, twice) it is not clear of noise.

**Term B: the step that failed most.** Forecast 62.9 us from exp of head 0 to the last scaling, at most 64.5; measured 76.8, and 70.4 with the clock mostly held (filled). VectorE's work was right: it is busy for 56.2 us of the 76.8, forecast 55.4 besides exp of head 0. What failed is its 5.6 us of waits; measured are 17.9. Two of the three pieces were mis-sized.

First, it put 1.5 for exp of the compressed scores. The wait for the compressed scores themselves (4.30) had no term, and that for their exp is 3.37: on ScalarE it stands behind exp of head 3, this behind the copies of head 1's transposes (a wait of 4.71), and these transposes come late, since half of the compressed scores and pair 2's scores now stand ahead of them. With clock and quarters mended and the softmax in step 2 (best_one_ahead), the loop takes the time forecast (63.1).

Second, the slack: 1.6 for "some" pairs. It is 6.5 in the change (4.8 for scores, 1.7 for exps), 4.3 in filled and 1.3 in best_one_ahead. So the size was right for a loop that starts in step and keeps its clock, and wrong for the one that was there. The working counted each engine's load and not the ring through three engines.

Third, the last head: 2.10 measured, 2.5 forecast, right.

**Term C: right place, wrong size.** The clock fell at 273.4, near 272 as said, but stayed low for 17 us, where half of 6.5 us of work was to be caught, and fell three times more. Its price in the changed order is 3.2 (filled against the change, medians, with intervals that overlap) to 7.2 (stages), forecast 2.4 with 4.2 as the bound. Fillers are worth 10 us on best, where there are 51 of them; the kernel before has 32 at other places, and they are worth nothing that can be measured.

**The rivals were taken for alternatives.** Late quarters, low clock in the loop (three stretches behind 290, the first of 10 us) and too little slack happened together, and the second comes at least in part of the third (fill_loop, own_step). The range ended at three low stretches and nothing else.

**What would show it:** the 11.5 us wait gone, yes; VectorE's longest wait for exp of head 0, no (4.1 as said, but 4.30 for the compressed scores); a clock of 0.50 between 272 and 290, yes; 2 to 3 us for the last head, yes; that exp between 270 and 272, no (273.59); 1 to 2 us for exp of the compressed scores, no (3.37); `out1` within 2 us of 342.3, no (355.95). "Wrong if" ScalarE waits over 1 us near 256 and the loop has microseconds at 0.50: both.

## What to carry to other kernels

An order that asks for an operand one step sooner is to be checked as a ring: sum what every engine does between the two uses of the same buffer, at full and at half clock, and compare it with the step of the engine that waits; each engine's load says nothing about it. Sort loads by who waits first, and count the bytes in the queue as well as the issues. When an engine's clock depends on its work, causes multiply: price each by taking one mend back from the mended version, as one at a time in the broken one they hide each other. And a price says what an edit is worth, not why: best_softmax_late cost what was expected, without the wait that was to explain it.

## What was not expected of the hardware

- TensorE can stay at 1.2 GHz while busy: 5.00 of 5.00 us at 0.50 in 280 to 285, with products of 30 columns and short transposes. In best the same 32 products of the compressed scores ran at 1.00 (3.65 us from 273.27), so the products alone don't bring the low clock. The Trainium skill ("TensorE: Matmul & The Clock Gate", Part 1) has activity release the throttle; in these 5 us, busy throughout by the profile, it was not released.
- 51 fillers, work that computes nothing, bought 10.2 us by the medians, 8.0 by the stage (best_bare against best).
- An identical part of the kernel, in which four or five transfers of `w_raw` are on the chain (2416 to 2581), takes 164.6 to 170.1 us from profile to profile, while 14 of the 20 parts into which ScalarE's table loads cut the span behind the stage repeat within 0.25 us.
